# One of four weight sums of each Strassen-like pair moves from VectorE to an adding DMA, and ten pairs of three FFNs take this form instead of eight

## What is computed

```
h = rms_norm(x, g)                      # 512 x 1024
gate, up = split(h @ w_gu)              # w_gu: 1024 x 5632, two halves of 2816
x = x + 0.5 * (silu(gate) * up) @ w_down   # w_down: 2816 x 1024
```

## Time and profile before

| | |
|---|---|
| time before, median of 3 runs | 2204.29 us (2204.25 to 2204.54) |
| the profiled execution's own time | 2204.55 us |
| its span (first to last instruction) | 2202.8 us |
| busy: PE, DVE, ACT, POOL | 99%, 66%, 45%, 7% |
| DMA engines' mean throughput | 99 GB/s |

### The profile page before, as it was taken

How to read it: one execution, slowest core, us unless ns; L and a number is a source line. 1 busy time by engine, 2 the same in 40 slices (tenths; PEclk the granted TensorE clock), 3 DMA queues, 4 the chain that set the end, 5 groups by cost and what they waited for, 6 DMA issues and landing times.

```text
span 2202.8 us, 28606 instructions
## 1 busy us (share of the span) xinstructions
PE 2186.0 (99%) x11576; PEld 1780.6 (81%) x11576; DVE 1450.1 (66%) x2245; ACT 988.9 (45%) x1542; POOL 154.7 (7%) x127
## 2 busy tenths in 40 slices
PE   9999999999999999999999999999999999999999
PEld 7889897777778898988898887777788888877777
DVE  6757476988657574766576677777575536555863
ACT  5424234667444242335333236777442222238672
POOL 3000003000120000030000021000310000020000
PEclk9999999999999999999999999999999999999999
DMA  6323234131225232232323232222144334242211
GB/s 196 115 77 115 77 104 131 40 97 59 77 76 193 79 110 82 96 115 77 115 93 118 87 105 78 79 75 85 58 153 143 125 115 134 92 133 77 77 58 39
DMA packets 201604, 217.77 MB, mean 99 GB/s; under 512 B 4777, under 2 KB 194345, under 8 KB 201473
## 3 DMA queue, kind: packets, MB, share of 16 engines
q1 hardware_dynamic: 194768, 193.48, 27.2%
q0 software_dynamic: 6560, 22.39, 3.0%
q10 hardware_dynamic: 144, 0.08, 0.0%
HBM read 213.79 MB, written 6.32 MB: 100 GB/s over the span
## 4 chain that ended last, share of the span: by engine, by line
PE 91%; DVE 5%; ACT 3%; issue 1%; DMA 0%; POOL 0%; SPq 0%; DVEq 0%; ACTq 0%
PE ps L1829 90%; DVE sb_wlo L1230 1%; PE ps L1833 1%; ACT sb_whi L715 1%; DVE sb_gla_ek L1535 0%; DVE sb_gla_eq L1538 0%; DMA sb_xT<-xT 0%; ACT sb_xh L715 0%; DVE sb_xT L1334 0%; ACT sb_hyb_th L715 0%; DVE sb_gla_xb L1530 0%; DVE sb_gla_cf L1527 0%; DVE sb_gla_d L1515 0%; DVE sb_xl L1252 0%; ACT sb_lnb L715 0%
## 5 line engine op out<-in xcount | busy, mean ns | idle before, releaser
L1829 PE MATMUL ps<-sb_xh,sb_whi 128*128 128x512 f32 (+1 forms) x2016 | 771.0, 382 | 1.8 <-DVE sb_xl L1618 0.9
L1829 PE MATMUL ps<-sb_xl,sb_whi 128*128 128x512 f32 (+1 forms) x2016 | 753.3, 375 | 0.3 <-DVE sb_xl L1252 0.3
L1829 PE MATMUL ps<-sb_xh,sb_wlo 128*128 128x512 f32 (+1 forms) x2016 | 751.2, 375 | 0.0
L715 ACT ACTIVATE sb_whi<-sb_raw 128x1024 fp32r<-128x1024 f32 (+1 forms) x376 | 378.3, 1016 | 411.0 <-PE ps L1829 403.7
L1230 DVE TENSOR_TENSOR sb_wlo<-sb_raw,sb_whi 128x1024 fp32r<-128x1024 f32 (+1 forms) x328 | 408.7, 1251 | 207.7 <-ACT sb_whi L715 205.0
L1829 PEld LDWEIGHTS ps<-sb_xh,sb_whi 128*128 128x128 f32 x2016 | 379.7, 188 | 86.5 <-issue 18.1
L1829 PEld LDWEIGHTS ps<-sb_xl,sb_whi 128*128 128x128 f32 x2016 | 380.0, 188 | 70.6 <-DVE sb_xl L1252 3.4
L1829 PEld LDWEIGHTS ps<-sb_xh,sb_wlo 128*128 128x128 f32 x2016 | 379.5, 188 | 69.5
L1829 PE MATMUL ps<-sb_ffn_ah,sb_whi 128*128 128x512 f32 x704 | 274.3, 390 | 0.0
L1829 PE MATMUL ps<-sb_ffn_ah,sb_wlo 128*128 128x512 f32 x704 | 273.9, 389 | 0.0
L1829 PE MATMUL ps<-sb_ffn_al,sb_whi 128*128 128x512 f32 x704 | 273.9, 389 | 0.0
(11 more groups left out here) (295 smaller groups left out, 2521.6 us busy)
## 6 DMA issues: line engine op xcount, KB each, us to landing
sb_raw<-ffn_w_gu SPq DMA_DIRECT2D x86, 1024.0 KB, 5.1
sb_raw<-ffn_w_down SPq DMA_DIRECT2D x32, 1024.0 KB, 5.4
sb_raw<-gla_w_in SPq DMA_DIRECT2D x12, 1024.0 KB, 5.4
sb_raw<-diff_w_in SPq DMA_DIRECT2D x12, 1024.0 KB, 5.1
sb_ada_raw<-w_ada POOLq DMA_DIRECT2D x12, 1024.0 KB, 6.3
sb_raw<-w_in SPq DMA_DIRECT2D x10, 1024.0 KB, 5.3
sb_raw<-ffn_w_down SPq DMA_DIRECT2D x12, 768.0 KB, 4.5
sb_raw<-gla_w_out SPq DMA_DIRECT2D x4, 1024.0 KB, 5.6
```

What stands on the lines that cost most here:

```text
L715: return e.activation(out, in_, func, bias=bias, scale=scale)
L1829: return e.matmul(out, lhsT, rhs, start=start, stop=stop, skip_group_check=skip)
```

## The change

Ten pairs of FFNs 0, 1 and 2 are fast, 6, 8, 9, 11, 12, 14, 16, 17, 19 and 20, where the even ones from 6 to 20 were. With quarters a, b (gate) and c, d (up), DVE made four sums: c+d, c+a in place of c, a+c+d, and a+b+c+d. Now POOL issues one DMA for each fast pair that adds a onto c in the raw buffer (128 partitions x 4 x 128 floats, 256 KB), and DVE makes three sums: (c+a)+d, that less a, and that plus b. DVE waits for the adding transfer's semaphore before its first sum, and so does ACT for the units made of the sums. Some semaphores are merged to make room for two new ones.

```diff
-FAST = (tuple(range(6, 22, 2)),) * 3 + ((),)
+FAST = ((6, 8, 9, 11, 12, 14, 16, 17, 19, 20),) * 3 + ((),)
...
                 lo_done(w, u - 1)
-                e.tensor_tensor(sums[:, 0:4, :], c_, d_, ALU.add).then_inc(sem["s_add"], 1)
-                w.wait_ge(sem["s_add"], 4 * i + 1)
-                e.tensor_tensor(c_, c_, a_, ALU.add).then_inc(sem["s_add"], 1)
-                e.tensor_tensor(sums[:, 4:8, :], sums[:, 0:4, :], a_, ALU.add).then_inc(sem["s_add"], 1)
-                w.wait_ge(sem["s_add"], 4 * i + 3)
+                w.wait_ge(sem[f"s_pre{i % 2}"], 16 * (i // 2 + 1))
+                e.tensor_tensor(sums[:, 4:8, :], c_, d_, ALU.add).then_inc(sem["s_add"], 1)
+                w.wait_ge(sem["s_add"], 3 * i + 1)
+                e.tensor_tensor(sums[:, 0:4, :], sums[:, 4:8, :], a_, ALU.subtract).then_inc(sem["s_add"], 1)
                 e.tensor_tensor(sums[:, 8:12, :], sums[:, 4:8, :], b_, ALU.add).then_inc(sem["s_add"], 1)
...
+            def gate_onto_up(f):
+
+                for u, (gate, up, i) in W.fast.items():
+                    if W.units[u][3] == "fa" and ffn_of(u) == f:
+                        off = W.units[u][1]
+                        for q in (gate, up):
+                            w.wait_ge(sem[f"raw{q % NRAW}"], 16 * (q // NRAW + 1))
+                        if i >= 2:
+                            w.wait_ge(sem["s_add"], 3 * i - 3)
+                        e.dma_start(raw[up % NRAW][:, 0:4, off:off + 128], raw[gate % NRAW][:, 0:4, off:off + 128],
+                                    accum_op=ALU.add).then_inc(sem[f"s_pre{i % 2}"], 16)
...
+            gate_onto_up(0)
             ffn_squares(0, KT)
             gla()
             out_squares(0)
             position_bias()
+            gate_onto_up(1)
             ffn_squares(1, KT)
+            gate_onto_up(2)
             ffn_squares(2, KT)
```

More of the change, by code:

```diff
@@ L386 @@
 f_g f_silu f_u f_p f_ah f_al f_x out_x
-s_add t_act t_vec f_join
-zero onehot bias_mm bias_rows bias_vec bias_rep
-ada0 ada1 ada_col ada_mm ada_add silu_c sp_act sp
+s_pre0 s_pre1 s_add t_act t_vec f_join
+zero bias_dma bias_mm bias_rows
+side0 side1 ada_col ada_mm ada_add silu_c sp_act sp
 g_in g_lr g_q g_k g_v g_vT g_vrow g_g g_silu g_zmm g_nb g_rbT g_zact g_z g_x0
 g_dk g_dq g_exp g_mk g_c g_x g_t g_mq g_level g_at g_atc g_o g_osq g_oss g_on g_y g_yhi g_ylo
-d_bias0 d_bias1 d_lam d_lam_mm d_lam_e d_neg d_qb_q d_qb_k d_sq_q d_sq_k d_ss d_qk_q d_qk_k
+d_lam d_lam_mm d_lam_e d_neg d_qb_q d_qb_k d_sq_q d_sq_k d_ss d_qk_q d_qk_k
 d_hi_q d_hi_k d_lo_q d_lo_k d_v d_vT d_vrow
 d_score d_max d_exp d_comb d_turn d_pt d_pv d_osq d_oss d_y d_yhi d_ylo
-h_in gs h_z h_hi h_conv0 h_conv h_gmm h_gates h_r h_i h_ix h_tanh h_a h_ln h_m h_sqrt h_one h_b h_scan
+gs h_z h_hi h_conv0 h_conv h_gmm h_gates h_r h_i h_ix h_tanh h_a h_ln h_m h_sqrt h_one h_b h_scan
 h_sq h_ss h_qk h_part h_other h_v h_vT h_vrow h_score h_max h_exp h_comb h_turn h_pt h_pv h_ya
@@ L731, in w_hi @@
                         if tag != "fa":
-                            w.wait_ge(sem["s_add"], 4 * i + {"fb": 2, "fc": 3, "fd": 4}[tag])
+                            w.wait_ge(sem["s_add"], 3 * i + {"fb": 1, "fc": 2, "fd": 3}[tag])
+                            w.wait_ge(sem[f"s_pre{i % 2}"], 16 * (i // 2 + 1))
                         act(whi[u % NSLOT][:, 0:nk, :], fast_source(u), ACT.Copy).then_inc(sem["w_hi"], 1)
@@ L1302, in ffn @@
                         if f == 1 and j == 6:
-                            w.wait_ge(sem["bias_vec"], 16)
+                            w.wait_ge(sem["bias_dma"], 32)
                         if fast:
@@ L1396, in ada_pair @@
                     rawt, acc = ada_raw[n % 2], ada_acc[n % 2]
-                    w.wait_ge(sem[f"ada{n % 2}"], 16 * (n // 2 + 1))
+                    w.wait_ge(sem[f"side{n % 2}"], 64 + 16 * (n // 2 + 1))
                     w.wait_ge(sem["silu_c"], 1)
@@ L1600, in diff @@
                             w.wait_ge(sem["d_score"], i + 1)
-                            w.wait_ge(sem[f"d_bias{h % 2}"], 16 * (h // 2 + 1))
+                            w.wait_ge(sem[f"side{h % 2}"], 16 * (h // 2 + 1))
                             if n >= 3:
@@ L1752, in hybrid @@
                         w.wait_ge(sem["h_score"], n + 1)
-                        w.wait_ge(sem["h_in"], 32)
+                        w.wait_ge(sem["g_in"], 64)
                         if n >= 3:
@@ L1921, in ffn @@
                         if f == 1 and j == 2:
-                            w.wait_ge(sem["onehot"], 16)
+                            w.wait_ge(sem["bias_dma"], 16)
                             w.wait_ge(sem["lnb"], ln_done(("norm", 2)))
@@ L2443, in position_bias @@
                 w.wait_ge(sem["x_lo"], 24)
-                e.dma_start(onehot[:, :], a["onehot"]).then_inc(sem["onehot"], 16)
+                e.dma_start(onehot[:, :], a["onehot"]).then_inc(sem["bias_dma"], 16)
                 w.wait_ge(sem["bias_rows"], 2)
-                e.dma_start(bias_vec, bias_rows[:, :]).then_inc(sem["bias_vec"], 16)
-                w.wait_ge(sem["bias_vec"], 16)
+                e.dma_start(bias_vec, bias_rows[:, :]).then_inc(sem["bias_dma"], 16)
+                w.wait_ge(sem["bias_dma"], 32)
                 e.dma_start(bias_rep.rearrange("h (r c) -> h r c", c=1024),
-                            bias_vec.unsqueeze(1).broadcast_to([8, 128, 1024])).then_inc(sem["bias_rep"], 16)
+                            bias_vec.unsqueeze(1).broadcast_to([8, 128, 1024])).then_inc(sem["bias_dma"], 16)
             def load_bias(h):
                 src = bias_rep[h, 127:127 + 128 * 1023].rearrange("(p c) -> p c", c=1023)[:, 0:896]
-                w.wait_ge(sem["bias_rep"], 16)
+                w.wait_ge(sem["bias_dma"], 48)
                 w.wait_ge(sem["x_lo"], 40)
@@ L2456, in load_bias @@
                     w.wait_ge(sem["d_max"], 8 * (h - 1))
-                e.dma_start(bt[h % 2][:, :], src).then_inc(sem[f"d_bias{h % 2}"], 16)
+                e.dma_start(bt[h % 2][:, :], src).then_inc(sem[f"side{h % 2}"], 16)
             def diff():
@@ L2470, in load_ada @@
                     w.wait_ge(sem["ada_col"], KT * (n - 1))
-                e.dma_start(ada_raw[n % 2][:, :, :], src).then_inc(sem[f"ada{n % 2}"], 16)
+                e.dma_start(ada_raw[n % 2][:, :, :], src).then_inc(sem[f"side{n % 2}"], 16)
             def hybrid():
                 w.wait_ge(sem["f_x"], last_x(3, KT - 1))
-                e.dma_start(causal[:, :], a["causal"]).then_inc(sem["h_in"], 16)
-                e.dma_start(lw, a["lru_w"]).then_inc(sem["h_in"], 16)
+                e.dma_start(causal[:, :], a["causal"]).then_inc(sem["g_in"], 16)
+                e.dma_start(lw, a["lru_w"]).then_inc(sem["g_in"], 16)
             e.dma_start(cst[:, :, :], a["cst"]).then_inc(sem["cst"], 16)
```

1 line of the change is left out of this document (added).

## The result

The changed kernel takes 2227.55 us (median of 4 runs, 2226.97 to 2228.09), the kernel before 2204.35 us in the same session: ratio 1.0105, 95% interval 1.0093 to 1.0117. The prediction was 2229 us, range 2220 to 2241, with 0.87 on slower. The profiled execution took 2227.93 us, its span is 2226.1 us.

What follows compares the result with a forecast made beforehand. PE was taken to bound the kernel. Profiled 2204.55 - 5.04 (six fast pairs) + 6.0 (waits side by side) + 23.65 (transfer behind the copy) = 2229.2, so 2229 us, 1.1% slower; range 2220 to 2241.

Steps and rivals of the forecast that it cites:

- What bounds the kernel: Whole kernel: PE, busy 99% of the span, so time is won only by giving PE less to do.
- The gain, 5.04 us: FFNs 0 to 2: six more fast pairs save PE 0.84 us each, if PE never waits.
- the waits side by side, 6.0 us: FFNs 0 to 2, pairs 12 and 20: DVE finishes fb late, so PE waits 1.0 us at each of six places.
- the handover to PE: After DVE's low part of fb in pairs 12 and 20: an estimated 0.25 us until PE goes on.
- The sum that goes: DVE in each of 30 fast pairs: 0.72 us less, worth nothing by itself, counting only where DVE is late.
- The adding transfer behind the copy: FFN 1, pair 6: the transfer waits in POOL's queue for the 4 MB copy, lands at 702.2, costs 23.65 us.
- rival 4: PE after its long idle stretch: half speed in fa of pair 6, 0 to 2 us more; part of main case (0.80).
- Rival 1: FFN 1, pair 6: transfer passes the copy, landing 3 to 4 us after issue; 2205.3 us, no change; chance 0.10.
- the two loads that went one behind the other: Two 1 MB loads issued back to back in POOL's queue, second 8.1 us: evidence that the adding transfer waits.
- Rival 2: The copy is passed and DVE keeps up in side by side pairs: 2199.3 us, 0.23% faster; chance 0.03.
- Rival 3: Adding transfers slow everywhere, over the 8 us that pair 14 leaves: 2245 us and above; chance 0.07.
- the wait for fc that I had counted on: FFN 1, pair 6: PE waits for fc until 8.9 us after the first sum, hiding 1.4 us of a cold fa.

Runs made afterwards that it cites:

- e9: e1 with nine fast pairs (6, 8, 9, 11, 13, 14, 16, 17, 19) in each of three FFNs: 2202.72 us.
- e1: The changed kernel with POOL issuing the adding transfer of FFN 1's pair 6 ahead of the 4 MB copy: 2205.21 us.
- e2: e1 with the eight fast pairs of before, the even ones from 6 to 20: 2204.47 us.
- e6: e1 with fast pairs 6, 8, 9, 11, 13, 15, 16, 17, 19, 21: 2209.95 us.
- e8: The kernel before, all four sums on DVE, with the ten fast pairs of e6: 2210.05 us.
- e3: The kernel before, all four sums on DVE, with the change's ten fast pairs: 2213.43 us.
- e7: The changed kernel with the 4 MB copy's outer dimension 128 rows instead of 8, still on POOL ahead of the transfer: 2219.84 us.
- e4: The changed kernel with the 4 MB copy in ACT's queue and pair 6's adding transfer in FFN 1 held until the copy runs: 2218.69 us.
- e5: e1 with fast pairs 13 and 14 in place of 11 and 12, listed as 6, 8, 9, 11, 13, 14, 16, 17, 19, 21: 2209.82 us.

## Why the prediction was right, step by step

- **What bounds the kernel.** PE. Shown by e9: three more fast pairs give 1.6 us of 3 x 0.84 = 2.5, and pair 14's waits of 0.25 us take 0.8 of the rest.
- **The gain, 5.04 us, and the waits side by side, 6.0 us.** The sum of both was to be +1.0; e1 has +0.9. The waits fell at fb of pairs 12 and 20, and nowhere else among the fast pairs. They are 0.95 each instead of 1.0. Two small errors nearly cancel. I put the handover to PE at 0.25. The low part of fb starts at 189.74 and lasts 1.22, so it ends at 190.96, 8.00 after the pair's start (the steps said 7.95), and PE goes on at 191.01: 0.05. So PE starts only 0.80 late. But the matmul behind it holds the next one back as well (191.24, 0.23 later instead of 0.12), for which I had no term, and the pair ends 0.96 late.
- **The sum that goes is worth nothing by itself, and counts where DVE is late.** Shown from both sides: 0.1 us in e2 and in e6 against e8, 8.2 us in e3 and 3.7 us in the nine pairs.
- **The adding transfer behind the copy.** Right in place and size, and in cause with one correction. I took the whole transfer to stand behind the copy. In the trace half of it passed, on the engines that the copy did not use, and only the other half waited; since DVE needs the last piece, the time is the same. It landed at 701.6 and not 702.2: the copy was issued 0.7 us later, took 26.7 instead of 27.5, and the transfer added 1.4 us behind it instead of 2.0. That this term came so close owes something to luck, since it was made for a whole transfer; in e7, with all pieces behind the copy, it was 3.2 us (landings at 690.5 and 693.7). From there both ends of the steps hold to 0.1: PE restarts 4.7 us after the landing (4.7 with the handover), pair 7 starts 17.84 after it (17.9). The steps between do not all hold: see rival 4. 22.65 us lost in the trace, 22.3 between the medians, 23.65 predicted: 0.65 of the difference to the trace is the earlier landing, 0.3 that pair 7 would have come so much later than before anyway.
- **Rival 1, the copy passed.** Out for the half that counted: it moved after 699, with the copy's end. e4 shows that it was the queue: with the same copy in another queue the transfer is not held until the copy's end. The rival's price was wrong too. Beside the copy and SP's load the transfer took 15.1 us (e4), not 3 to 4. And the two loads that went one behind the other told of each engine's order in one queue, not of a transfer that uses engines which the copy leaves free.
- **Rival 2, DVE keeps up.** Out for the ten pairs; nearly true of the nine (e9), where fb was late only by pair 14's 0.25 us.
- **Rival 3, adding slow everywhere.** Out. 4.3 us alone; the nearest row, a plain load, had 3.0, and pair 14's spare time of 8 us held it. Of DVE's 30 first sums (L1245) only the one of FFN 1's pair 6 waited for a DMA.
- **Rival 4, PE cold.** The clock did fall, and cost nothing, but not in the way that I had worked out. Fa took 4.95 us (706.24 to 711.19) instead of 2.88, the clock being back at 1.00 before its last matmuls. The low part of fc was ready at 710.3 (709.06 and 1.23 us), so the wait for fc that I had counted on never came: PE went from fa to fc without a pause. The wait for fb hid the loss: PE was through with fd at 715.5 and still had to wait until 716.41. The windows after the wait:

```profile
707.00:711.00 4.00, 4.00 (x22) 4.00 (x21) 2.36 (x4) 2.10 (x3) 0.00 (x0) 0.53 0.00 0
711.00:715.00 4.00, 4.00 (x35) 4.00 (x35) 2.38 (x4) 2.11 (x3) 0.00 (x0) 1.00 0.00 0
```

The granted clock is 0.53 from 707 to 711 (1.2 GHz for most of it), after 19.4 us without a matmul, and 1.00 from 711 on. The Trainium skill, "TensorE: Matmul & The Clock Gate", Part 1, says that an idle array drops to 1.2 GHz; by this the trace agrees.

What stays open: why the first packet of e4's adding transfer came 5.9 us after its issue; why the copy on 16 engines gained only a third; and why the clock falls after some of the 1.8 us waits and not after others.

## What to carry to other kernels

Before you hand work to a DMA queue, list what stands ahead of it in that queue at each use, and on how many engines. Twenty-nine of thirty transfers here took a few microseconds and one took 27.1, and a median hides that one. A mean busy share (66% of DVE) tells nothing of a helper's slack: take it through one period of the pattern, with what its results are due for, and place the denser work where the next need is late, not as the last pair ahead of a consumer. The value of taking work off an engine depends on the order around it: the same sum was worth 0, 3.7 and 8.2 us.

## What the runs showed of the hardware that I had not expected

- Of an adding transfer issued right behind a 4 MB copy in the same queue, half of the pieces moved within 4.1 us of the issue and half after the copy, 24.5 us and more behind the issue. With the copy on all 16 engines (e7) none moved before 688.4, near its end. So the order in a queue held on each DMA engine for itself.
- In its own queue a 256 KB adding transfer beside a 4 MB copy took 15.1 us, against 4.3 alone. On the engines that three queues shared, each queue got one packet per turn, whether it was of 512 bytes, 1 KB or 4 KB.
- SP's load of 1 MB beside the copy took 17.8 us in the kernel before, 18.0 in the changed one and 20.4 in e4, where such loads take 5.4 as a rule. In the kernel before PE has no wait beside it (640 to 760).
- A broadcast copy of 4 MB took 26.7 us with an outer dimension of 8 and 17.5 with one of 128.
- After waits of 1.8 us the granted clock was 1.2 GHz in two of three places in e5 and in one of three in e6 and in e8, for some 3 us of matmuls each time. I had counted on that only after long idle stretches.
